# MLA heads in pairs with values token by token, and retention's rotary step on VectorE with values token by token

## The reference

```python
# MLA, 8 heads: 64 channels without rotation and 32 rotary ones for queries and keys, 64 for values
q  = (rmsnorm(c_q, g_cq) @ w_uq)            # 768 -> 8 x (64 + 32)
kv = (rmsnorm(c_kv, g_ckv) @ w_ukv)         # 256 -> 8 x (64 + 64)
q_rope = apply_rope(q[..., 64:]); k_rope = apply_rope(k_rope_raw)   # k_rope: one for all heads
s = (q_nope . k_nope + q_rope . k_rope) * 96 ** -0.5                # causal
o = softmax(s) @ v
# retention, 4 heads: q, k of 64 channels, v of 128
q = apply_rope(q); k = apply_rope(k) * 64 ** -0.5
scores = q . k * decay;  o = scores @ v     # the kernel takes the whole sequence at once
# apply_rope: concat(x1 * cos - x2 * sin, x2 * cos + x1 * sin) of the two halves x1, x2
```

## Time and profile before

| | |
|---|---|
| median of 3 runs | 1353.59 us (1353.09 to 1354.54) |
| time of the profiled execution | 1356.47 us |
| its span of instructions | 1354.7 us |
| PE busy, DVE busy, ACT busy, POOL busy | 97%, 50%, 48%, 53% |
| chain that ended last: PE, DVE, ACT | 91%, 4%, 3% |

### The profile page before, as it was taken

One profiled execution on the slowest core, in us unless ns is written; L12 is line 12 of the kernel. 1 busy time (PEld: TensorE's weight loads), 2 busy tenths in 40 slices (PEclk: granted clock), 3 DMA queues, 4 the chain that ended last, 5 costly groups with the idle time before them and its releaser, 6 DMA issues.

```text
span 1354.7 us, 17300 instructions
## 1 busy us (share of the span) xinstructions
PE 1308.1 (97%) x5938; PEld 1036.3 (77%) x5938; DVE 678.0 (50%) x1111; ACT 645.9 (48%) x995; POOL 724.1 (53%) x1495
## 2 busy tenths in 40 slices
PE   5999999999999999999979999999999999999996
PEld 2878887787777777788857888778777777778884
DVE  6766776434564344353355677642355423433333
ACT  3366655434554244354335566554455434444431
POOL 3365456674334554576647555576433454556662
PEclk7999999999999999999989999999999999999998
DMA  9321223342223333242222211233211222232221
GB/s 368 120 85 63 70 72 93 132 133 90 82 83 105 114 98 117 89 136 94 94 70 94 78 63 63 71 111 123 86 62 63 83 89 86 78 102 86 93 94 63
DMA packets 40792, 131.89 MB, mean 97 GB/s; under 512 B 5248, under 2 KB 5376, under 8 KB 39424
## 3 DMA queue, kind: packets, MB, share of 16 engines
q1 hardware_dynamic: 30336, 111.57, 24.3%
q10 hardware_dynamic: 10368, 19.21, 4.8%
HBM read 128.13 MB, written 2.10 MB: 96 GB/s over the span
## 4 chain that ended last, share of the span: by engine, by line
PE 91%; DVE 4%; ACT 3%; POOL 1%; issue 1%; DMA 1%; ACTq 0%; DVEq 0%
PE ps_st L774 23%; PE ps_st L776 23%; PE ps_st L775 23%; PE ps_o L796 5%; PE ps_s L827 3%; PE ps_s L874 2%; PE ps_s L898 2%; PE ps_w L883 1%; PE ps_misc L791 1%; POOL w_lo L646 1%; PE ps_misc L782 1%; PE ps_w L729 1%; DMA cur<-params_cur 1%; PE ps_s L829 1%; PE ps_misc L787 1%
## 5 line engine op out<-in xcount | busy, mean ns | idle before, releaser
L646 POOL TENSOR_TENSOR w_lo<-raw,w_hi 128x128 fp32r<-128x128 f32 x1472 | 711.6, 522 | 589.9 <-ACT w_hi L952 589.7
L774 PE MATMUL ps_st<-h_hi,w_hi 128*128 128x512 f32 x984 | 401.0, 407 | 2.5 <-POOL w_lo L646 2.0
L776 PE MATMUL ps_st<-h_hi,w_lo 128*128 128x512 f32 x984 | 384.2, 390 | 0.0
L775 PE MATMUL ps_st<-h_lo,w_hi 128*128 128x512 f32 x984 | 383.5, 390 | 0.0
L774 PEld LDWEIGHTS ps_st<-h_hi,w_hi 128*128 128x128 f32 x984 | 185.2, 188 | 47.4 <-issue 6.8
L775 PEld LDWEIGHTS ps_st<-h_lo,w_hi 128*128 128x128 f32 x984 | 185.3, 188 | 42.0 <-issue 6.2
L776 PEld LDWEIGHTS ps_st<-h_hi,w_lo 128*128 128x128 f32 x984 | 184.9, 188 | 39.8
L952 ACT ACTIVATE w_hi<-raw 128x1024 fp32r<-128x1024 f32 x184 | 193.3, 1051 | 27.9 <-PE ps_st L776 24.7
L974 ACT ACTIVATE gate_t<-gate_x 128x512 f32<-128x512 f32 x80 | 50.5, 631 | 247.6 <-DVE gate_x L1273 247.5
L1273 DVE TENSOR_SCALAR gate_x<-ps_st 128x512 f32<-128x512 f32 x79 | 54.5, 690 | 220.3 <-PE ps_st L776 219.9
L976 ACT ACTIVATE gate_t<-gate_t,cs 128x512 f32<-128x512 f32 x80 | 57.9, 724 | 2.6
(11 more groups left out here) (283 smaller groups left out, 2003.8 us busy)
## 6 DMA issues: line engine op xcount, KB each, us to landing
raw<-w_stream SPq DMA_DIRECT2D x184, 512.0 KB, 3.4
mod_w<-w_mod ACTq DMA_DIRECT2D x64, 256.0 KB, 2.7
pro_w<-w_mod_first SPq DMA_DIRECT2D x8, 1024.0 KB, 14.0
x<-x_t SPq DMA_DIRECT2D x4, 512.0 KB, 7.4
ret_decay<-decay ACTq DMA_DIRECT2D x2, 1024.0 KB, 4.7
out_t<-o_t SPq DMA_DIRECT2D x8, 256.0 KB, 2.1
raw_extra<-w_stream SPq DMA_DIRECT2D x2, 512.0 KB, 20.1
cs<-cst SPq DMA_DIRECT2D x1, 836.0 KB, 7.5
```

The lines of the kernel that those rows point to most:

```text
L646: ins = nc.gpsimd.tensor_tensor(lo[:, r], whole[:, r], hi[:, r].bitcast(F32), ALU.subtract)
L774: nc.tensor.matmul(dst[0:m, :], wh, hi, start=(k == 0), stop=False)
L775: nc.tensor.matmul(dst[0:m, :], wh, lo, start=False, stop=False)
L776: last = nc.tensor.matmul(dst[0:m, :], wl, hi, start=False, stop=(k == nk - 1))
```

## The change

MLA heads are taken in pairs. An item `mq` j holds the 64 plain query channels of heads 2j and 2j+1 in one tile and their keys in another (4 items of 24 matmuls). An item `mr` j holds the rotary query channels of four heads (2 items of 18 matmuls). One item `mv` makes the values of all heads with the tokens on the partitions: the token blocks of `ckv_hi` are the weights and the projection's columns are streamed, in four tiles of 6 matmuls, so nothing is turned over. The rotary step becomes one multiplication of 128 rows and four of 32 rows that read the other half from other partitions. The query rotation reads PSUM and is written at the step `item mr`; the two key tiles are copied out of PSUM by DVE at `item mq`; the rotated keys are written once, at `kr_rope`. Scores contract over 128 rows instead of 96. Retention's `rq` and `rk` are rotated by DVE straight from PSUM in six instructions, and `rv` is made token by token in four items that add into four banks. The swap matmuls, the transposes of values and ACT's copies of them are gone. The masks of one mixer and some scratch tiles are laid out otherwise.

```diff
-    for it in ma[1:-3]:
+    for it in ma[1:-4]:
         item(*it)
-    item("mla", 0)
-    item(*ma[-3])
-    s.append(("mla_qk", 0))
-    item("mla", 1)
-    item(*ma[-2])
+    for it, other in zip(ma[-4:], (("mr", 0), ("mv", 0), ("mq", 0))):
+        item(*it)
+        item(*other)
     item(*ma[-1])
-    item("bg", 0)
+    behind = [("bg", 1), ("mq", 1), ("mr", 1), ("mq", 2), ("bg", 2), ("mq", 3), ("bg", 3), ("rq", 0)]
     for h in range(MLA_HEADS):
 
         s += [("mla_s", h, 3), ("mla_s", h, 2)]
         if h:
             s.append(("mla_pv", h - 1))
-        if h + 1 < MLA_HEADS:
-            s.append(("mla_qk", h + 1))
         else:
-            s.append(("ret_rope", "rq", 0))
-        if h % 2 == 1 and h + 1 < MLA_HEADS:
-            item("bg", (h + 1) // 2)
+            item("bg", 0)
         s += [("mla_t", h, 3), ("mla_t", h, 2), ("mla_s", h, 1), ("mla_s", h, 0)]
-        item(*(("mla", h + 2) if h + 2 < MLA_HEADS else ("rq", h + 2 - MLA_HEADS)))
+        item(*behind[h])
         s += [("mla_t", h, 1), ("mla_t", h, 0)]
...
                     elif kind == "mla_s":
                         h, qi = s[1:]
-                        if e.new(q_ready, h + 1):
-                            pe.wait_ge(q_ready, e.at(q_ready, h + 1))
...
+                        if e.new(q_ready, h // 2 + 1):
+                            pe.wait_ge(free[e.bank_of((("mq", h // 2), 0))], e.use(free, (("mq", h // 2), 0)))
+                            pe.wait_ge(free[e.bank_of((("mq", h // 2), 1))], e.use(free, (("mq", h // 2), 1)))
+                            pe.wait_ge(q_ready, e.at(q_ready, h // 2 + 1))
...
+                def ret_rope(key, dst):
+
                     dve.wait_ge(full[e.bank_of(key)], e.use(full, key))
                     ps = bank[e.bank_of(key)]
...
+                    half = RET_DK // 2
+                    V.tensor_tensor(t1[:], ps[:], cos_ret[:], ALU.mult)
+                    for a in range(0, P, half):
+                        first = a % RET_DK == 0
+                        b = slice(a + half, a + RET_DK) if first else slice(a - half, a)
+                        last = V.scalar_tensor_tensor(t2[a:a + half, :], ps[b, :], -1.0 if first else 1.0, sin_ret[b, :],
+                                                      ALU.mult, ALU.mult)
+                    last.then_inc(free[e.bank_of(key)], 1)
...
+                def mla_rope(t):
+
+                    V.tensor_tensor(t1[:], t[:], trig[:], ALU.mult)
+                    for a in range(0, P, ROPE):
+                        b = a + ROPE if a % (2 * ROPE) == 0 else a - ROPE
+                        last = V.tensor_tensor(t2[a:a + ROPE, :], t[b:b + ROPE, :], sin_mla[b:b + ROPE, :], ALU.mult)
+                    return last
...
+                    elif kind == "mr":
+                        dve.wait_ge(full[e.bank_of((it, 0))], e.use(full, (it, 0)))
+                        mla_rope(bank[e.bank_of((it, 0))]).then_inc(free[e.bank_of((it, 0))], 1)
+                        dve.wait_ge(free[e.bank_of((it, 0))], e.use(free, (it, 0)))
+                        V.tensor_tensor(sq_sum[:], t1[:], t2[:], ALU.add).then_inc(dve_link, 1)
+                        dve.wait_ge(dve_link, e.made(dve_link))
+                    elif kind == "mq":
+                        r = slice(0, NOPE) if j % 2 == 0 else slice(NOPE, P)
+                        V.tensor_scalar(mla_q[NOPE:P, 0, :], sq_sum[r, :], MLA_SCALE, None, ALU.mult)
+                        V.tensor_scalar(mla_q[0:NOPE, 1, :], sq_sum[r, :], MLA_SCALE, None, ALU.mult).then_inc(q_ready, 1)
+                        dve.wait_ge(full[e.bank_of((it, 1))], e.use(full, (it, 1)))
+                        ps = bank[e.bank_of((it, 1))]
+                        V.tensor_copy(mla_kv[0:NOPE, 0, :], ps[0:NOPE, :])
+                        V.tensor_copy(mla_kv[NOPE:P, 1, :], ps[NOPE:P, :]).then_inc(free[e.bank_of((it, 1))], 1)
...
                     elif kind == "kr_rope":
...
+                        V.memset(v_ones[:, :, :, 1, :], 1.0)
+                        mla_rope(k_rope).then_inc(dve_link, 1)
+                        dve.wait_ge(dve_link, e.made(dve_link))
+                        V.tensor_tensor(mla_kv[0:NOPE, 1, :], t1[0:NOPE, :], t2[0:NOPE, :], ALU.add)
+                        V.tensor_tensor(mla_kv[NOPE:P, 0, :], t1[NOPE:P, :], t2[NOPE:P, :], ALU.add).then_inc(k_ready, 1)
```

More of the change, by code:

```diff
@@ L242, in build_uses @@
             use("misc", ("ssq",))
+        elif kind == "item" and s[1] == "rv":
+            if s[2] == 0:
+                for t, b in enumerate(RV_BANK):
+                    use(b, ("rv", t))
         elif kind == "item" and layer == 0 and s[1:] in BATCH:
@@ L245, in build_uses @@
         elif kind == "item":
-            for t in range(len(tiles_of(s[1:]))):
+            for t in range(outs_of(s[1:])):
                 use(STREAM[out % 2], (s[1:], t))
@@ L619, in _ @@
                 sp.dma_start(cos_ret[half, :], trig[RET_DK // 2:RET_DK, :]).then_inc(tables_in, 16)
+            for q in range(0, P, ROPE // 2):
+                first = P - ROPE // 2 if q % (2 * ROPE) < ROPE else P - ROPE
+                sp.dma_start(sin_mla[q:q + ROPE // 2, :], trig[first:first + ROPE // 2, :]).then_inc(tables_in, 16)
             for layer in range(DEPTH):
@@ L622, in _ @@
                     load(layer, i)
+                    if layer == 0 and i == len(BATCH) + RING:
+                        sp.wait_ge(tables_in, TABLES_IN)
+                        for q in (0, ROPE, 3 * ROPE):
+                            sp.dma_start(trig[q:q + ROPE, :], trig[2 * ROPE:3 * ROPE, :]).then_inc(tables_mla, 16)
             for j in range(DT):
@@ L777, in item, with values_item, retention_values @@
                         done(last, (it, t))
+                def values_item(it):
+                    i = ITEM_AT[it]
+                    pe.wait_ge(w_lo_ready, e.at(w_lo_ready, i + 1))
+                    _, w_h, w_l = weights(layer, i)
+                    for t in range(CH):
+                        dst = take((it, t))
+                        r = slice(t * P, (t + 1) * P)
+                        for k in range(CKT):
+                            hi, lo = moving("mv", 0, k)
+                            wh, wl = w_h[:, k * CH * P:(k + 1) * CH * P], w_l[:, k * CH * P:(k + 1) * CH * P]
+                            nc.tensor.matmul(dst[:], hi[:, r], wh, start=(k == 0), stop=False)
+                            nc.tensor.matmul(dst[:], hi[:, r], wl, start=False, stop=False)
+                            last = nc.tensor.matmul(dst[:], lo[:, r], wh, start=False, stop=(k == CKT - 1))
+                        done(last, (it, t))
+                def retention_values(j):
+                    i = ITEM_AT[("rv", j)]
+                    pe.wait_ge(w_lo_ready, e.at(w_lo_ready, i + 1))
+                    _, w_h, w_l = weights(layer, i)
+                    for k in range(DT // CH * j, DT // CH * (j + 1)):
+                        a = k % (DT // CH) * CH * P
+                        wh, wl = w_h[:, a:a + CH * P], w_l[:, a:a + CH * P]
+                        for t in range(CH):
+                            dst = take(("rv", t)) if k == 0 else bank[e.bank_of(("rv", t))]
+                            r = slice(t * P, (t + 1) * P)
+                            nc.tensor.matmul(dst[:], h_hi[:, k, r], wh, start=(k == 0), stop=False)
+                            nc.tensor.matmul(dst[:], h_hi[:, k, r], wl, start=False, stop=False)
+                            last = nc.tensor.matmul(dst[:], h_lo[:, k, r], wh, start=False, stop=(k == DT - 1))
+                            if k == DT - 1:
+                                done(last, ("rv", t))
+                    if j < CH - 1:
+                        last.then_inc(rv_read, 1)
                 def transposes(key, src):
@@ L783, in transposes @@
                     done(last, key)
-                def swap_halves(key, perm, src, rows):
-                    dst = take(key)
-                    done(nc.tensor.matmul(dst[0:rows, :], perm[0:rows, 0:rows], src, start=True, stop=True), key)
                 def column_sums(key, src):
@@ new lines, in item @@
+                        A(mla_q[NOPE:P, 1, :], src[NOPE:P, :], ACT.Copy, scale=MLA_SCALE).then_inc(free[e.bank_of((it, 0))], 1)
+                    elif kind == "mv":
+                        for t in range(CH):
+                            copy_out((it, t), values_of(t), bank[e.bank_of((it, t))][:].rearrange("p (a b m) -> p a b m", a=PAIRS, b=2))
+                    elif kind == "rq" and j == 0:
+                        act.wait_ge(full[e.bank_of((it, 0))], e.use(full, (it, 0)))
+                        act.dma_start(ret_decay[:], decay).then_inc(decay_in, 16)
+                    elif kind == "rv" and j == CH - 1:
+                        for t in range(CH):
+                            copy_out(("rv", t), ret_v[:, :, t, :], bank[RV_BANK[t]][:].rearrange("p (a b) -> p a b", b=P))
@@ L1531, in first_norm @@
                 def first_norm():
```

(1 more changed line is left out.)

216 lines of the change are left out of this document (93 added, 123 removed).

## The result

The changed kernel takes 1369.65 us in the median of four executions (1367.47 to 1372.47), the kernel before beside it 1354.07: an estimated ratio of 1.0106, 95% interval 1.0083 to 1.0129. Four more executions, later, gave 1368.3 against 1354.67 (1.0088, 1.0063 to 1.0113). It is slower; the medians differ by 13.6 and 15.6 us, where 5.9 were forecast. The profiled execution took 1367.5 us, its span 1365.7 against 1354.7, 11.0 more.

What follows compares the result with a forecast made beforehand. PE, busy 97% of the span, was taken as the bound. 37.9 us off against 41.8 of new waits gave +3.9, plus 2 for the clock: 5.9 on the median, 1359.5 us, range 1349 to 1367.

Steps and rivals of the forecast that it cites:

- Direction and size: Whole kernel: slower with chance 0.57, same 0.27, faster 0.16; 5.9 us more on the median.
- What goes: PE in both layers: removed matmuls, value transposes, swaps and head 0's wait take 37.9 us off.
- `mr` 1: Head 2: `mla_pv` waits 5.2 us a layer for DVE's copy of block 1 behind tail and rotary step.
- `mq`: Heads 1, 3, 5: the next head's scores wait 1.5 us each for DVE's copies, 4.4 a layer.
- `bg`: Heads 0, 4, 6: PE waits for ACT's copy of block 0 behind the gate, 1.6, 2.4 and 2.4 us a layer.
- Rotary key: `kr_rope`: longer DVE work delays `pa` 0 and merge item 3's weights, 3.7 us a layer in two pieces.
- `mr` 0: `pa` 2: its second tile waits 1.2 us a layer for the bank that the rotary step holds.
- The clock: Behind the two `mr` 1 waits: TensorE at half speed costs 2 us for the pair, between 0 and 5.
- Balance: Rival, chance 0.20: rotary products overlap at 0.61 and the clock stays up, so waits balance the work, 1354 us.
- earlier tails: Rival, chance 0.18: tails of head pairs come 2.5 us earlier against the item, shortening waits, 1346 us.
- Streaming matmuls at 0.25: Rival, sharing 0.12 with late weights: 240 matmuls streaming projection columns cost 0.25 each, adding 5 us, 1365.
- Late weights in the heads: Rival, sharing 0.12 with dearer streaming: weights of one item a head come 1 us late, 16 us in all, 1375.

Runs made afterwards that it cites:

- experiment 9: Kernel before with only retention's half of the change, `rq` 0's rotary step moved behind the maxima of head 7's first two blocks: 1350.0 us, ratio 0.9961.
- experiment 3: The changed kernel run once more, unaltered, to see whether span and mean granted clock move together: 1368.3 us.

## Why the prediction was right, and where it failed

- **Direction and size.** Slower was right, at 0.57. The time, 1369.65, lies 2.7 above the upper end, and the loss is 13.6 to 15.6 us instead of 5.9.
- **What goes, 37.9.** Right in the matmuls (184 instructions fewer, 0.2265 to 0.2275 apart, shown by experiment 9 for retention's half). Scores over 128 rows cost what those over 96 did (1.02 listed for the two of 512 columns in both). The waits removed were 2.2 instead of 3.8: the wait for `gate` did not vanish in others but grew to 1.2 in layer 1.
- **`mr` 1, 5.2 forecast.** Measured 5.09 and 5.10, by the chain that the prediction wrote down: tail, four products 0.70 apart, sum, copy.
- **`mq`, 8.8.** Measured 8.5: 1.53 at heads 1 and 5, 1.20 at head 3.
- **`bg`, 12.8.** Measured 8.4: 2.02 instead of 2.4, 1.19 instead of 1.6, and one of four missing, behind the wait for `gate` just ahead.
- **Rotary key, 7.4.** Measured 5.7 more than before. The first piece came as forecast, at `pa` 0 (3.9 and 3.1, of which 1.3 and 0.4 stood there before); the second was 0.85 in layer 1, and in layer 0 the half clock hid it.
- **`mr` 0, 2.4.** Measured 1.9.
- **The clock, 2 of 0 to 5.** This is the term that was mis-sized. In the profile it is 9.3. Over all executions: the median one of the changed kernel has a clock of 0.9735 and a span of 1367.9, so 72 us at half clock, the kernel before 0.985 and 1352.6, so 41; 31 us by 0.31 is 10. The step that failed is "The waits at `mr` 1 are as long; I take 2 us for the pair of them": the pair cost 4.4, and it looked for a fall only behind waits as long as the one between the layers. But the clock fell behind the rotary key's waits, behind waits of 2.0 us and behind one of 1.22 too, at one in one execution and at another in the next; these four (1.4 + 1.8 + 1.8 + 1.6) are 6.6. The experiment that fills all waits gives 7 to 8.5 us for the clock without any of these estimates.
- **The rivals.** Balance and earlier tails are out: the clock did not stay up, and `y_lo` ended 6.7 us after its item began, as before. Streaming matmuls at 0.25 are out by the 0.2265. Late weights in the heads did not come.

Without the clock the forecast was +3.9; the run with all waits filled has +6.7, 1.3 of which are the weights of merge item 3 that came late only there, and the sum over the profiles has +0.8. The waits, which took most of the working, were the sound part of it: each was found at its place. But their sum was 41.8 forecast against 37.1 measured (34.7 + 2.4), and what goes was 1.6 too high; these two errors hid some 3 us of the clock's error, which is luck.

## What to carry to other kernels

Where an instruction leaves a busy TensorE for an engine that is half idle, price what stands behind the new instruction in that engine's order: six instructions of 0.7 us ahead of a copy of 0.42 or an addition of 0.16 cost 3.8 to 5.1 us here, as much as 17 to 22 matmuls. And price each wait that you put into a dense stretch with the half clock that may follow it, short ones too: here 8.4 us of waiting were worth 13 to 15 in the median of ten executions, and 9 in one of them. Both are mended by order alone, so when a change that removes work comes out slower, list what the new instructions were put ahead of before giving it up.

## What the hardware did that was not expected

- The granted clock went to 1.2 GHz behind waits of 2.0 us, with one of 1.2 to 1.5 some 13 us ahead of each, in a stretch that was otherwise dense, and not each time (experiment 3). By the spans of 26 executions of the kernel before, one us at half clock goes with 0.31 us of time. The Trainium skill, page "TensorE: Matmul & The Clock Gate", section "HAM oscillation — how this bites in real kernels", ties the fall to gaps longer than these; the trace shows it behind shorter ones too, and the measurement decides.
- The rotary products that read `k_rope` from SBUF while POOL was working took 0.856 us each, those that read the bank 0.686, of the same size. The kernel before shows the same for products with both inputs in SBUF: 0.686 where POOL's instruction was not yet running as they began, 0.837 where it was (its two lines below, `mla_q` and `k_rope`). While the products of the changed kernel ran, eight of POOL's subtractions took 7.68 us; in the kernel before, eight at the same place took 5.47, and elsewhere 3.87, where DVE was busy for less than half of the time:

```profile
L1298 DVE TENSOR_TENSOR t<-ps_st,sin_mla x16: 679/686/697, 288.1 to 1018.5; 32x512 f32<-32x512 f32 x16
L1298 DVE TENSOR_TENSOR t<-k_rope,sin_mla x8: 845/856/865, 240.9 to 904.4; 32x512 f32<-32x512 f32 x8
...
L1254 DVE TENSOR_TENSOR t<-mla_q,trig x16: 686/686/689, 294.2 to 1058.6; 32x512 f32<-32x512 f32 x16
L1254 DVE TENSOR_TENSOR t<-k_rope,trig x2: 837/837/837, 242.9 to 897.3; 32x512 f32<-32x512 f32 x2
```

```profile
239.55 7.68 POOL L669 TENSOR_TENSOR w_lo<-raw,w_hi 128x128 fp32r<-128x128 f32 x8 [5.56 <-ACT w_hi L1004]
...
354.07 3.87 POOL L669 TENSOR_TENSOR w_lo<-raw,w_hi 128x128 fp32r<-128x128 f32 x8 [8.86 <-ACT w_hi L1004]
```

  The Trainium skill, page "SBUF — State Buffer", section "SBUF: two separate sides", says that VectorE with two inputs from SBUF and GpSimd take turns at a shared pair of ports; the trace agrees in that both engines are slower side by side.
